# Decoder trunk on one core: first norm gain as a scale per feature on transposed x, x transposed into four banks, first weight slot in two quarters and a half

## What is computed

```
def rmsnorm(x, g):
    y = x * rsqrt(mean(x * x, axis=-1) + 1e-6)
    return y * g
def short_conv_mixer(h, w_in, w_conv, w_out):
    bg, cg, xv = split(h @ w_in, 3)
    return (bg * causal_dwconv(cg * xv, w_conv)) @ w_out
h = rmsnorm(x, norm_mix[0])
x = x + short_conv_mixer(h, a_w_in[0], a_conv[0], a_w_out[0])
```

## Time and profile before

| | before |
|---|---|
| median of 3 runs | 601.89 us |
| span of the profiled execution | 600.3 us |
| TensorE busy (matmul) | 591.0 us, 98% |
| VectorE busy | 386.3 us, 64% |
| ScalarE busy | 288.4 us, 48% |
| GpSimd busy | 10.5 us, 2% |
| moved by DMA | 108.02 MB, mean 180 GB/s |

### The profile page before, as it was taken

One profiled execution on the slowest core, in us unless ns is written; L12 is line 12 of the kernel. 1 busy time (PEld: TensorE's weight loads), 2 busy tenths in 40 slices (PEclk: granted clock), 3 DMA queues, 4 the chain that ended last, 5 costly groups with the idle time before them and its releaser, 6 DMA issues.

```text
span 600.3 us, 10234 instructions
## 1 busy us (share of the span) xinstructions
PE 591.0 (98%) x4239; PEld 558.0 (93%) x4239; DVE 386.3 (64%) x450; ACT 288.4 (48%) x325; POOL 10.5 (2%) x22
## 2 busy tenths in 40 slices
PE   8999999999999999999999999999999999999995
PEld 6999998999999999999899999889999999999994
DVE  4686767576555656567786677785666655655554
ACT  5534353565543554445455455644754443454431
POOL 2000000000000000000100000000000000000001
PEclk9999999999999999999999999999999999999999
DMA  8996466356664555655656544353565665554001
GB/s 276 344 297 204 159 235 218 115 194 211 211 199 156 199 162 193 208 160 192 211 158 216 189 141 141 141 210 106 170 233 164 206 210 163 186 175 174 0 1 70
DMA packets 80912, 108.02 MB, mean 180 GB/s; under 512 B 1833, under 2 KB 71665, under 8 KB 80882
## 3 DMA queue, kind: packets, MB, share of 16 engines
q1 hardware_dynamic: 80160, 104.97, 53.1%
q10 hardware_dynamic: 722, 2.63, 1.2%
HBM read 106.54 MB, written 1.05 MB: 179 GB/s over the span
## 4 chain that ended last, share of the span: by engine, by line
PE 95%; DMA 1%; DVE 1%; issue 1%; ACT 1%; POOLq 0%; POOL 0%; SPq 0%; DVEq 0%; ACTq 0%
PE proj L784 22%; PE proj L786 22%; PE proj L785 22%; PE acc L826 8%; PE acc L828 8%; PE acc L830 8%; PE tr L840 1%; PE acc L786 1%; PE acc L785 1%; PE acc L784 1%; DMA xs<-in_x 1%; PE tr L785 1%; PE tr L786 1%; PE tr L784 1%; PE tr L889 0%
## 5 line engine op out<-in xcount | busy, mean ns | idle before, releaser
L522 DVE TENSOR_TENSOR w_lo<-raw,w_hi 128x2048 fp32r<-128x2048 f32 x94 | 215.1, 2292 | 84.7 <-ACT w_hi L324 83.4
L784 PE MATMUL proj<-hA_hi,w_hi 128*128 128x256 f32 x864 | 245.0, 284 | 0.0
L786 PE MATMUL proj<-hA_hi,w_lo 128*128 128x256 f32 x864 | 244.6, 283 | 0.0
L785 PE MATMUL proj<-hA_lo,w_hi 128*128 128x256 f32 x864 | 244.5, 283 | 0.0
L324 ACT ACTIVATE w_hi<-raw 128x2048 fp32r<-128x2048 f32 x94 | 179.4, 1909 | 53.3 <-PE acc L830 41.1
L784 PEld LDWEIGHTS proj<-hA_hi,w_hi 128*128 128x128 f32 x864 | 165.8, 192 | 0.7
L785 PEld LDWEIGHTS proj<-hA_lo,w_hi 128*128 128x128 f32 x864 | 165.8, 192 | 0.7
L786 PEld LDWEIGHTS proj<-hA_hi,w_lo 128*128 128x128 f32 x864 | 165.8, 192 | 0.0
L609 DVE SCALAR_TENSOR_TENSOR scratch<-proj,f_par,scratch 128x255 f32<-128x255 f32 (+1 forms) x80 | 33.1, 476 | 48.2 <-ACT scratch L391 48.2
L391 ACT ACTIVATE scratch<-proj,f_par 128x256 f32<-128x256 f32 x40 | 20.4, 559 | 69.7 <-PE proj L786 69.7
L826 PE MATMUL acc<-w_hi,kq_hi 128*128 128x512 f32 x160 | 49.6, 391 | 0.0
(11 more groups left out here) (127 smaller groups left out, 661.5 us busy)
## 6 DMA issues: line engine op xcount, KB each, us to landing
raw<-in_ffn_w_up SPq DMA_DIRECT2D x44, 1024.0 KB, 5.1
raw<-in_ffn_w_down SPq DMA_DIRECT2D x22, 1024.0 KB, 4.9
raw<-in_a_w_in SPq DMA_DIRECT2D x11, 1024.0 KB, 10.8
raw<-in_w_kv SPq DMA_DIRECT2D x8, 1024.0 KB, 5.3
raw<-in_a_w_out SPq DMA_DIRECT2D x4, 1024.0 KB, 4.8
raw<-in_b_w_q SPq DMA_DIRECT2D x4, 1024.0 KB, 5.2
raw<-in_b_w_o SPq DMA_DIRECT2D x4, 1024.0 KB, 4.9
raw<-in_a_w_in SPq DMA_DIRECT2D x2, 512.0 KB, 7.8
```

Source lines behind the costliest of these rows:

```text
L522: dve.tensor_tensor(wlo, raw[:, s % RAW, :], whi.bitcast(F32), ALU.subtract).then_inc(w_lo_ready, 2 if s + 1 in AHEAD else 1)
L784: pe.matmul(dst, sh, mh, start=first, stop=False)
L785: pe.matmul(dst, sh, ml, start=False, stop=False)
L786: return pe.matmul(dst, sl, mh, start=False, stop=last)
```

## The change

Four things are changed, all in the opening; slots 1 and later, and everything behind them, keep their code except that counts of `h_hi_ready`, `h_lo_ready` and `x_T` are moved on.

1. The first gain is no longer spread over partitions and multiplied in when x is normalised. It is loaded as eight rows of 128, transposed by TensorE to one column per feature block (`gain0`, 128x8), and applied as a scale per partition to the transposed x: by ScalarE when it makes `hA_hi`, by VectorE when it makes `hA_lo`. Both now work on one feature block at a time, eight instructions of 128x128 per row tile instead of two of 128x512. The normalise is x times `rstd` alone.
2. x is transposed into four PSUM banks, two feature blocks in each, and each pair is signalled by itself. TensorE's matmuls of slot 0 wait for each block.
3. Slot 0 comes in two quarters and a half, each with its own landing and split. Its half and x1 are issued by ScalarE's queue instead of SP's.
4. The order is changed: `warm(8)` stands ahead of the first transposes; the second row tile's transposes stand behind all eight blocks of the first row tile; ScalarE squares the second row tile behind slot 0's split, and `hi(1)` stands behind `hA_hi` of the second row tile.

```diff
@@ sync: SP @@
-            sp.dma_start(xs[:, 1, :], x_rows[:, 1, :]).then_inc(x1_in, 16)
-            halves = raw[:, 0, :].rearrange("p (g k n) -> p g k n", g=2, n=256)
-            for g, landing in enumerate((first_landed, landed[0])):
-                sp.dma_start(halves[:, g], in_rows[:, 4 * g:4 * g + 4, D:D + 256]).then_inc(landing, 16)
+            for g in range(2):
+                sp.dma_start(first_raw(g), first_src[g]).then_inc(first_landed[g], 16)
@@ tiles @@
+        first_pieces = [slice(0, COLS // 4), slice(COLS // 4, COLS // 2), slice(COLS // 2, COLS)]
+        first_banks = [tr[0][:], tr[1][:], acc[1][0][:], acc[1][1][:]]
+        gain0_rows_T = bank[1][:, 0:KD]
+        def first_T(k):
+            return first_banks[k // 2][:, P * (k % 2):P * (k % 2) + P]
@@ scalar @@
+            def first_h_hi(t, h):
+                act.wait_ge(gain0_ready, 1)
+                for k in range(4 * h, 4 * h + 4):
+                    if k % 2 == 0:
+                        act.wait_ge(x_T, 4 * t + k // 2 + 1)
+                    act.activation(hA_hi[:, k, P * t:P * t + P], first_T(k), ACT.Identity,
+                                   scale=gain0[:, k:k + 1]).then_inc(h_hi_ready, 1)
...
+            def first_w_hi(g):
+                act.wait_ge(*((first_landed[g], 16) if g < 2 else (landed[0], 16)))
+                part = first_pieces[g]
+                act.activation(split_slot(0)[0][:, part], raw[:, 0, part],
+                               ACT.Copy).then_inc(first_hi if g < 2 else w_hi_ready, 1)
-            act.dma_start(gain[0:1, :], GAIN[0].rearrange("(a n) -> a n", a=1)).then_inc(gain_in, 16)
-            for t in range(2):
-                for h in range(2):
-                    square(0, t, h)
-            first_half_hi()
+            act.dma_start(gain[0:KD, 0:P], GAIN[0].rearrange("(k n) -> k n", n=P)).then_inc(gain_in, 16)
+            act.dma_start(xs[:, 1, :], x_rows[:, 1, :]).then_inc(x1_in, 16)
+            act.dma_start(first_raw(2), first_src[2]).then_inc(landed[0], 16)
             for h in range(2):
-                h_hi(0, 0, h)
-            act.wait_ge(landed[0], 16)
-            act.activation(w_hi[:, 0, COLS // 2:], raw[:, 0, COLS // 2:], ACT.Copy).then_inc(w_hi_ready, 1)
+                square(0, 0, h)
+            first_w_hi(0)
+            first_w_hi(1)
+            for h in range(2):
+                first_h_hi(0, h)
+            first_w_hi(2)
+            for h in range(2):
+                square(0, 1, h)
+            for h in range(2):
+                first_h_hi(1, h)
             hi(1)
-            for h in range(2):
-                h_hi(0, 1, h)
             hi(2)
@@ vector @@
+            def first_h_lo(t, h):
+                for k in range(4 * h, 4 * h + 4):
+                    if k % 2 == 0:
+                        dve.wait_ge(h_hi_ready, 8 * t + k + 2)
+                    dve.scalar_tensor_tensor(out=hA_lo[:, k, P * t:P * t + P], in0=first_T(k),
+                                             scalar=gain0[:, k:k + 1],
+                                             in1=hA_hi[:, k, P * t:P * t + P].bitcast(F32),
+                                             op0=ALU.mult, op1=ALU.subtract).then_inc(h_lo_ready, 1)
+            dve.wait_ge(gain0_T, 1)
+            dve.tensor_copy(gain0[:], gain0_rows_T).then_inc(gain0_ready, 1)
+            dve.wait_ge(gain0_ready, 1)
             mean_square(0, 0)
             normalise(0, 0)
+            first_w_lo(0)
+            first_h_lo(0, 0)
+            first_w_lo(1)
+            first_h_lo(0, 1)
+            first_w_lo(2)
             mean_square(0, 1)
...
             normalise(0, 1)
...
+            for h in range(2):
+                first_h_lo(1, h)
             lo(1)
             lo(2)
@@ tensor @@
+                    if s == 0:
+                        pe.wait_ge(h_lo_ready, KD * t + k + 1)
+                        if t == 0 and k in (0, 2, 4):
+                            pe.wait_ge(*((w_lo_ready, 1) if k == 4 else (first_lo, k // 2 + 1)))
...
+            def first_transposes(t):
+                for k in range(KD):
+                    if k % 4 == 0:
+                        pe.wait_ge(normed_ready, step4(0, t, k // 4))
+                    if t and k % 2 == 0:
+                        pe.wait_ge(h_lo_ready, k + 2)
+                    last = pe.transpose(first_T(k), normed[:, t, P * k:P * k + P], ident[:])
+                    if k % 2:
+                        last.then_inc(x_T, 1)
...
-            for h in range(2):
-                pe.matmul(acc[1][h][:], ones[:], gain[0:1, 512 * h:512 * h + 512],
-                          start=True, stop=True).then_inc(gain0_spread, 1)
-            transposes(0, 0)
+            pe.transpose(gain0_rows_T, gain[0:KD, 0:P], ident[0:KD, 0:KD]).then_inc(gain0_T, 1)
             warm(8)
-            project_rows(0, 0, 0, 0, lambda: transposes(0, 1))
-            project_rows(0, 0, 1, 0).then_inc(slot_done, 1)
+            first_transposes(0)
+            project_rows(0, 0, 0)
+            first_transposes(1)
+            project_rows(0, 0, 1).then_inc(slot_done, 1)
```

More of the change, by code:

```diff
@@ L106, in build @@
         ident = sb("ident", [P, P])
-        ones = sb("ones", [1, P])
+        gain0 = sb("gain0", [P, KD])
         par_rows = sb("par_rows", [P, 3, P])
@@ L138, in build @@
         gain_in = sem("gain_in")
-        gain0_spread = sem("gain0_spread")
+        gain0_T = sem("gain0_T")
+        gain0_ready = sem("gain0_ready")
         gained = sem("gained")
@@ L216, in step4, with h_step, first_raw @@
             return 4 * n + 2 * t + h + 1
+        def h_step(n, t, h):
+            return step4(n, t, h) + 12 if n else 8 * t + 4 * h + 4
+        first_pieces = [slice(0, COLS // 4), slice(COLS // 4, COLS // 2), slice(COLS // 2, COLS)]
+        first_src = [in_rows[:, 0:2, D:D + 256], in_rows[:, 2:4, D:D + 256], in_rows[:, 4:8, D:D + 256]]
+        first_banks = [tr[0][:], tr[1][:], acc[1][0][:], acc[1][1][:]]
+        gain0_rows_T = bank[1][:, 0:KD]
+        def first_T(k):
+            return first_banks[k // 2][:, P * (k % 2):P * (k % 2) + P]
+        def first_raw(g):
+            return raw[:, 0, first_pieces[g]].rearrange("p (k n) -> p k n", n=256)
         block = ctx.enter_context(nc.Block())
@@ L294, in _ @@
             pool.memset(minus_half[:], -0.5).then_inc(zeroed, 1)
-            pool.memset(ones[:], 1.0).then_inc(zeroed, 1)
-            pool.wait_ge(zeroed, 3)
+            pool.wait_ge(zeroed, 2)
             pool.affine_select(out=ident[:], in_=ident[:], compare_op=ALU.not_equal, fill=1.0, base=0,
@@ L553, in normalise @@
                     cols = slice(512 * h, 512 * h + 512)
-                    if n in (0, 3):
-                        dve.wait_ge(*((gain_in, 16 * 4) if n else (gain0_spread, h + 1)))
+                    if n == 0:
+                        dve.tensor_scalar(normed[:, t, cols], xs[:, t, cols], rstd[:, t:t + 1], None,
+                                          ALU.mult).then_inc(normed_ready, 1)
+                    elif n == 3:
+                        dve.wait_ge(gain_in, 16 * 4)
                         dve.scalar_tensor_tensor(out=normed[:, t, cols], in0=xs[:, t, cols], scalar=rstd[:, t:t + 1],
-                                                 in1=gain[:, cols] if n else acc[1][h][:],
-                                                 op0=ALU.mult, op1=ALU.mult).then_inc(normed_ready, 1)
+                                                 in1=gain[:, cols], op0=ALU.mult, op1=ALU.mult).then_inc(normed_ready, 1)
                     else:
@@ L700, in normal_probs, with first_w_lo @@
                                       ALU.mult).then_inc(probs_ready, 1)
+            def first_h_lo(t, h):
[6 more added lines that the diff above has]
+                                             op0=ALU.mult, op1=ALU.subtract).then_inc(h_lo_ready, 1)
+            def first_w_lo(g):
+                dve.wait_ge(*((first_hi, g + 1) if g < 2 else (w_hi_ready, 1)))
+                part = first_pieces[g]
+                dve.tensor_tensor(split_slot(0)[1][:, part], raw[:, 0, part], split_slot(0)[0][:, part].bitcast(F32),
+                                  ALU.subtract).then_inc(first_lo if g < 2 else w_lo_ready, 1)
+            dve.wait_ge(gain0_T, 1)
+            dve.tensor_copy(gain0[:], gain0_rows_T).then_inc(gain0_ready, 1)
+            dve.wait_ge(gain0_ready, 1)
             mean_square(0, 0)
             normalise(0, 0)
+            first_w_lo(0)
[3 more added lines that the diff above has]
+            first_w_lo(2)
             mean_square(0, 1)
-            dve.wait_ge(first_hi, 1)
-            dve.tensor_tensor(w_lo[:, 0, 0:COLS // 2], raw[:, 0, 0:COLS // 2], w_hi[:, 0, 0:COLS // 2].bitcast(F32),
-                              ALU.subtract).then_inc(first_lo, 1)
-            h_lo(0, 0)
             normalise(0, 1)
-            dve.wait_ge(w_hi_ready, 1)
-            dve.tensor_tensor(w_lo[:, 0, COLS // 2:], raw[:, 0, COLS // 2:], w_hi[:, 0, COLS // 2:].bitcast(F32),
```

(16 more changed lines are left out.)

14 lines of the change are left out of this document (5 added, 9 removed).

## The result

The changed kernel takes 607.19 us (median of four runs: 605.03, 606.77, 607.62, 607.74) against 601.87 us beside it (601.01 to 602.15). The ratio is 1.0084, with a 95% interval of 1.0065 to 1.0103. It is slower by 5.3 us, where +2.4 was forecast, and it lies outside the range. The run with the profile is the fastest of the four, 605.03; its mean granted clock is 0.996, those of the others 0.993, 0.988 and 0.988. That difference turns out to be more than a third of the matter.

A forecast was written before the change was run, and what follows sets the result against it. TensorE, busy 98%, bounds the kernel as one rigid block, shifted by slot 1's start. The chain p 9.0, W 12.7, W + 9.75 = 22.45 against 20.09 gave +2.4 us: 601.9 + 2.4 = 604.3, range 602.4 to 606.5.

The forecast's parts named there:

- p: Landing of slot 0's second quarter, from which the chain was counted: taken as 9.0 us, bounds 7.9 and 10.9.
- W: End of ScalarE's first_w_hi(2), the split of slot 0's half: p + 3.7 = 12.7 us.
- What bounds, and the 0.23 us of slack: TensorE from about 15.5 us is one rigid block; slot 1's w_lo is ready only 0.23 us ahead of use.
- Transfers: Opening loads on two queues: second quarter at 9.0 us, dip filling gives up to 0.5 us, slot 1's transfer unchanged.
- Small instructions: ScalarE's eight first_h_hi per row tile: 0.26 us apart, bounds 0.16 to 0.40, 2.1 us for eight.
- the prediction's other estimate, 0.29: Spacing of first_h_hi by the skill's instruction costs: 0.29 us, making the sum 0.5 us more over both row tiles.
- Rival 2: Small ScalarE instructions only 0.16 us apart, together with an early landing: -1.0 us, 600.9, faster; chance 0.06.
- Second row tile, moved steps: Squares, normalise, transposes and hi(1) queue behind W: lo(1) done at W + 9.6, slot 1 at 22.45 us.
- The first transposes: First row tile on TensorE: transposes still start at about 7.3 us, first pair done at 7.9, nothing won.
- Rival 3, the clock: TensorE's clock falls in the opening's idle gaps, slowing k = 4 to 7 and slot 1: together +4.5, 606.4; chance 0.15.
- Rivals 1, 2 and 4: The first of these: both queues fill the dip, p falls to 7.4 or below, +0.6 us, 602.5; chance 0.14.
- rival 4: ScalarE's transfers stand behind SP's: p = 7.9, half lands at 10.9, +1.7, 603.6; chance 0.65 shared with the forecast.

The follow-up runs named there:

- aw_oneq: The changed kernel with TensorE's opening holes filled by unused matmuls and all transfers issued by SP in the order of before: 604.52 us, ratio 1.0051.
- a_oneq: The changed kernel with all transfers issued by SP in the order of before, TensorE's holes left as they are: 606.29 us, ratio 1.0085.
- b_both: The kernel before with row tile 1's transposes behind all eight blocks and hi(1) behind the second row tile's h_hi: 604.62 us, ratio 1.0042.
- a_again: The changed kernel run once more, unedited: 606.57 us, ratio 1.0093.
- a_warm: The changed kernel with unused matmuls on the identity put into TensorE's holes of the opening: 605.01 us, ratio 1.0064.
- b_late_T: The kernel before with only row tile 1's transposes moved behind all eight blocks of the first row tile: 603.93 us, ratio 1.0035.
- b_best: The kernel before with x1 on ScalarE's queue and the second row tile's normalise ahead of the first w_lo: the same time as before.

## Why the prediction was wrong

The step that failed is the clock: the sum put it at nothing, on an argument that covered short holes only, and it cost 1.6 us at the median and up to 3.3. The direction was right, and so was the chain that the sum follows; one of its terms, the landing of the second quarter, was 0.7 us too small. With that one put right alone the forecast would have been 605.0, which is the time of the profiled run and lies inside the range. By its own steps, with p = 9.68 and so W = 13.34 in the profiled execution:

```
step                                forecast       measured
second quarter landed, p            9.0            9.68
first_h_hi apart                    0.26           0.25
end of first_w_hi(2), W             p + 3.7        p + 3.66
end of first_w_lo(2)                W + 1.25       W + 1.4
k = 4 to 7 done                     W + 2.8        W + 3.1
first_h_hi(1) starts                W + 3.3        W + 3.6
hi(1) starts                        W + 5.4        W + 5.6
lo(1) done                          W + 9.6        W + 9.9
slot 1 starts                       22.45          23.26
TensorE's hole ahead of it          2.5            2.2
```

- *What bounds, and the 0.23 us of slack:* right. Everything behind 15.5 us moved as one block, 3.2 us at slot 1 and 3.26 up to the end.
- *Transfers:* this term was mis-sized, +0.7 us. I let the second queue fill the dip of the earlier trace rows and took p ahead of the 9.4 of before. The dip was filled, as the busy time by stretch of the changed kernel shows:

```profile
3.50:4.50 1.00, 1.00 (x5) 0.90 (x5) 0.30 (x2) 0.74 (x3) 0.00 (x0) 1.00 1.03 303
```

That is 303 GB/s in place of 162 (two profiles with one queue show 168, `aw_oneq`, and 266, `a_oneq`, so it isn't the second queue's doing alone). But the gain went to what ScalarE's queue carries: x1 landed at 6.41 instead of 7.89, the half at 9.96 instead of 10.91, and the second quarter at 9.68, not at 9.0. The Trainium skill ("DMA: Bandwidth & Descriptors", Issuing engines are not separate DMA queues) says that the transfers interleave on the same engines. The 9.68 lies in the 9.4 to 10.9 that the prediction had worked out by that. With one queue the second quarter landed at 9.04 and 9.13 in the order of the change (9.33 to 9.81 in five profiles with two), and `aw_oneq` is 0.5 us faster.
- *Small instructions:* 0.25 us apart, as forecast with 0.26; the prediction's other estimate, 0.29, was too high. Rival 2 needed 0.16 and falls with that.
- *Second row tile, moved steps:* right in kind and within 0.2 us in size. `b_both` puts 2.8 us on two of the moved lines alone.
- *The first transposes* were to start at 7.3 and started at 8.10, since x0's second half landed at 5.89 instead of 4.50. It cost nothing, because the second quarter came later still.
- *Rival 3, the clock:* this is the step that failed; the sum had no term for it. It had a chance of 0.15 because the 0.57 us hole of the earlier trace rows had done nothing; but the change makes holes of 2 us and more, of which no row of before told anything, and that argument held for short holes only. The clock fell in both profiles of the changed kernel as it stands, and the granted clocks of nearly all its runs say so. Its price was somewhat low: 1.1 us for k = 4 to 7 with the transposes, where twelve matmuls at 0.1 more each make 1.2 without any transpose (measured 1.4 from k = 4 to the first `first_h_hi`, 3.43 us in `a_again` against 1.99 in the profile of the result; slot 1 is 1.6 later, 0.13 of it by the landing), and 1.0 in slot 1 (measured 1.5, `a_oneq`). With the sizes as measured the chain plus one of the two makes 604.3 + 0.7 + 0.1 + 1.6 = 606.7, already beyond the 606.5 at which my range ended.
- *Rivals 1, 2 and 4* did not come: the chain starts at the second quarter (9.68) and not at the first transposed pair, and the half landed at 9.96, right behind the second quarter and not 3 us after it, as rival 4 has it.

What stays open is why the low clock lies now on one step, now on another, from one execution to the next, and with it which runs pay 0, 1.6 or 3 us. No run varied that alone, and the slower three of the result's four runs have no profile: that the clock makes their 1.7 to 2.7 us over the first is read from their granted clocks and from `a_again` and `a_warm`. The gap between the 607.19 of the result and the 606.57 of `a_again` on another chip is within what that does.

## What to carry to other kernels

A step moved behind others in an engine's queue costs what those others wait for as well as what they take: here the eight small instructions took 2.0 us where the two large ones took 1.0, and what they waited for, the transposes after the whole first row tile, cost 2.1 by itself. Follow every path into the next slot, not only the longest: `b_late_T` missed because slot 0's own second row tile was left out. Where a change opens holes of 2 us and more in sparse work ahead of dense work, price the lower clock as the likely case, and look in all runs' granted clocks, since the one profiled execution can be the one in which it fell where it costs nothing. Filling such holes with unused matmuls helps only if the filling ends before the work is ready; sixteen of them behind slot 0 cost 1.9 us or more.

## What the runs showed of the hardware

- The granted clock fell to the lower level in an opening in which no single hole of the result, `a_again` and `a_oneq` was longer than 2.9 us, and TensorE had worked nearly without a gap from 1.6 to 7.0 us or later before them. The stretches behind show 0.54 (the result), 0.50 (`a_again`) and 0.56 (`a_oneq`), each in another place: on k = 0 to 3, on k = 4 to 7 and on slot 1. The Trainium skill ("TensorE: Matmul & The Clock Gate", Why this matters for your kernels) warns of idle gaps between bursts of matmuls, and the trace agrees in kind.
- Over all profiles: the seven that have a hole of 2.1 to 3.3 us behind the clock's first rise show a fall, and the nine with no hole longer than 1.5 us there show none (`b_best` has 2.35 us ahead of its first rise, and none). Which hole a fall follows is not settled by its length: in `a_oneq` the one of 2.84 us ahead of k = 0 left the clock up, and the one of 2.16 ahead of slot 1 is followed by the low clock. No run has one such hole alone with the rest filled.
- With one queue x0's second half landed at 4.1 to 5.2 us (eight profiles), with two at 4.7 to 7.4 (nine). The largest of these, in `b_best`, has slot 1 start 1.7 us late in the profiled execution, which was the slowest of its twelve (603.81).
- A ScalarE instruction of 128 columns with its scale in memory and a VectorE one with a scalar and a second tensor both take 0.25 to 0.26 us apart in a row of four.
